# Seams between the sublayers of a fused two-block transformer kernel: the order of sums, squares and splits

## Chip, core and metric

The kernel runs on one core of one Trainium2 chip. The metric is device time in microseconds (us), the median over several executions. TensorE is called PE here, VectorE DVE, ScalarE ACT, GpSimd POOL and SyncE SP, as the profile does.

## What is computed

A residual stream `h` of 256 tokens by 1024 columns goes through two blocks of two layers each, all in 32-bit precision. Cut to what matters:

```python
# first block, per layer l of 2
h = h + 0.5 * swiglu(rmsnorm(h, g0), Wg, Wu, Wd)          # feed-forward, 1024 -> 2816 -> 1024
h = h + mixer_1(rmsnorm(h, g1))                           # four attentions, gated and merged
h = h + 0.5 * swiglu(rmsnorm(h, g2), Wg, Wu, Wd)
h = rmsnorm(h, final_g)                                   # after layer 1
# second block, per layer i of 2
h = h + 0.5 * rmsnorm(swiglu(rmsnorm(h, g0), ...), g1)
h = h + rmsnorm(mixer_2(rmsnorm(h, g2)), g3)              # i=0 dilated attention, i=1 retention
h = h + 0.5 * rmsnorm(swiglu(rmsnorm(h, g4), ...), g5)
```

So there are twelve normalised inputs, p = 0 to 11, and twelve sublayers. A **seam** here is the stretch from the last matmul of one sublayer to the full run of the next; seam p is named by the norm in it. Norms 0, 2, 3, 5, 6, 8, 9, 11 feed a feed-forward (FFN); 1, 4 feed the first block's mixer, 7 the dilated attention, 10 the retention. Seams 1, 3, 4 follow an FFN of the first block, 6 follows it with the final norm between, 7, 9, 10 follow an FFN of the second block, 2 and 5 a mixer of the first block, 8 and 11 a mixer of the second.

## The kernel before, in words

**Weights.** 299 slots of 128 x 3072 floats stream through a ring of four slots (`ring`), loaded by SP; a slot is loaded again once `ring_used` has counted its last use. A matmul at single-pass speed takes operands in a short float form, so each weight w is split in two: the high part `ring_hi` (a rounding copy on ACT, `take_high`, L1444, in an FFN L1480 and L1492) and the low part `ring_lo` = w - high, written over the weight itself (a subtraction on DVE, `take_low` L1772, in an FFN L1821 and L1841). PE multiplies high by high, high by low and low by high. `ring_hi` has two places. Semaphores `hi_ready` and `lo_ready` count split slots in order; PE waits for `lo_ready` in `split_weights` (L796).

**FFN.** Each of 22 slots holds a tile of gate, of up and of down weights. For slot g PE does `gate_up` (L847, 32 matmuls into banks 4 to 7 by turns) and `down` of slot g-1 (L861, 12 matmuls, accumulated over all slots into banks 0 to 3; bank n holds token half n // 2, column half n % 2). ACT and DVE turn each gate/up result into the hidden tile in between (`tile` in ACT's `ffn`, L1470, and in DVE's, L1814). At its end `tile(g)` also splits the first two thirds of slot g+2, so the last two tiles split those of the next sublayer's first two slots: L1492 on ACT, L1841 (128 x 2048) on DVE, which waits for it. If the next sublayer is a mixer, the last third of these two slots is split by `take_high_back` (L1450) and `take_low_back` (L1778), inside the norm.

**Norm.** The gain-scaled, not yet normalised input is transposed; the row factor r = 1/sqrt(mean of squares) is applied to the results later. In the order of each engine's queue:
- DVE `add_output` (L1851; first block) adds banks 0, 1, 2, 3 to `h` (L1857), 512 columns of one token half at a time, each counted in `h_ready`. In the second block ACT squares each bank (`square_outputs`, L1506), DVE multiplies it by the gain (L1872), sums the squares per token half (L1863, `mean_of_output`), POOL takes the power -0.5 for each half (L2430, `output_roots`), and DVE adds to `h` (L1878) in the order of banks 0, 1, 2, 3. The final norm does the like in place (L2043).
- PE `norm` (L821) transposes `h` by column pairs kp = 0 to 3, 16 transposes (L831); kp 0 and 1 wait for `h_ready` at 4p-1 (three adds), kp 2 and 3 for 4p.
- ACT `norm` (L1452) squares token half 0 (L1457, 128 x 1024), makes the high part of the input in eight copies (L1466), then squares half 1.
- DVE `norm` (L1781) makes the low part in eight steps (L1789), splits the back third of the first slot if there is one, waits for both squares, makes the mean `h_sq` (L1794), waits for POOL's root `r_tok` (L2424), builds two diagonals `diag` (L1797), and splits the back third of the second slot.
- PE `root_row` (L838) multiplies a block of ones by `diag`, which gives r as a row in all partitions; DVE `copy_row` (L1802) copies it. In an FFN it stands after the first `gate_up`, into bank 3, then come four fills of banks 0 to 3 with zeros (L883), the fourth after a wait for that copy.

In the two mixers of the second block projection pieces go to banks 6 and 7 by turns (`tile_piece`, L1201). Piece g waits until piece g-2 has been copied out (`piece_bank_2`, L1196), and the copies need the row of r; `root_row` stands after the second piece.

Of the kernel before, what the change touches and what calls it, by code (L numbers as in the profile page):

```python
# [15 lines left out]
P = 128  # L16
SEQ = 256
# [149 lines left out]
def build(nc, stream, x_rows, norm_gT_2, gains_2, table_2, pick_2, ret_const, decay, norm_gT, mla_gT, sinks, posT, lam, subln, table_1, consts, flip_dram, pick_1, out):  # L167

    ctx = ExitStack()
    with ctx:  # L170
# [40 lines left out]
        diag = sb("diag", [P, TT, P])  # L211
# [115 lines left out]
        diag_ready = sem("diag_ready")  # L327
# [108 lines left out]

        def mix_slot(l):
            return l * C_LAYER + C_FFN
# [25 lines left out]

        def dilated_copy(g):


            n, bank = (g - PIECES_DIL) % 8, ps[:, 6 + g % 2, :]
# [16 lines left out]
        def retention_copy(g):  # L485
            what, bank = RET_PIECES[g - PIECES_RET], ps[:, 6 + g % 2, :]
# [295 lines left out]
        def _(pe):  # L782
# [38 lines left out]
            def norm(p, banks):  # L821
# [16 lines left out]
            def root_row(p, bank):  # L838


                pe.wait_ge(diag_ready, p + 1)
                pe.matmul(ps[:, bank, 0:SEQ], ones[:, :], diag[:, :, :].rearrange("p t c -> p (t c)"),
                          start=True, stop=True).then_inc(row_psum, 1)

            def ffn(f, c0, p, last_of_all=False):

                def gate_up(c, t, i=None, first=False):  # L847
                    split_weights(c, i)
                    for part in range(2):
                        for k in range(KD):  # L850
# [10 lines left out]
                def down(c, t, i=None, final=False):  # L861
                    v = FT * f + (c - c0) + 1
                    pe.wait_ge(hidden_ready, v if i is None else NS * i + v)
                    for tt in range(TT):
                        for half in range(2):
                            cols = slice(2 * D + half * 512, 2 * D + half * 512 + 512)
                            x_hi, x_lo = (x[:, t % 2, tt * P:(tt + 1) * P] for x in (hid_hi, hid_lo))
                            for x, w in ((x_hi, high(c)), (x_hi, low(c)), (x_lo, high(c))):
                                last = pe.matmul(ps[:, tt * 2 + half, :], x, w[:, cols], start=False,  # L869
                                                 stop=final and x is x_lo, skip_group_check=True)  # L870
                            if final:
                                last.then_inc(part_ready, 1)
# [1808 lines left out]
```

## Time and profile before

| | us |
|---|---|
| median of 3 runs | 2924.21 (2923.81 to 2926.12) |
| the profiled execution: its time | 2919.25 |
| the profiled execution: its span | 2917.4 |
| PE busy | 2802.2 (96%) |
| DVE / ACT / POOL busy | 1788.1 (61%) / 1342.5 (46%) / 88.6 (3%) |
| mean granted clock of PE | 0.992 |

Durations below come from the profiled execution. Its times are counted from the start of the span; the 1.85 us between span and time lie around it. PE runs at a granted clock of 1.00 (2.4 GHz) or 0.50 (1.2 GHz) in the windows read here.

### The profile page before, as it was taken

How to read it: one execution, taken by the hardware profiler on the slowest of the kernel's cores; microseconds unless marked ns; L12 is line 12 of the kernel's file. 1: busy time of each engine (PE TensorE's matmuls, PEld its weight loads, DVE VectorE, ACT ScalarE, POOL GpSimd, SP SyncE). 2: the span in 40 equal slices, each digit the busy share in tenths (PEclk: the TensorE clock that was granted, in tenths of full speed). 3: DMA queues.
4: the chain of work that ended last, by engine and by line, in shares of the span. 5: the costliest groups of instructions: out<-in, count | busy, mean ns of one | idle time of the engine just before them, and what ended most of it. 6: DMA issues, size and time to landing. Idle time of an engine off the chain costs nothing.

```text
span 2917.4 us, 41161 instructions
## 1 busy us (share of the span) xinstructions
PE 2802.2 (96%) x16502; PEld 2388.7 (82%) x16502; DVE 1788.1 (61%) x2753; ACT 1342.5 (46%) x1937; POOL 88.6 (3%) x135
## 2 busy tenths in 40 slices
PE   7999999999999999999999989998999998999998
PEld 6888988688788888877878879996887887986787
DVE  5665566366666656645666665554666666652665
ACT  4553444254554444424545544444545554451444
POOL 1000000000000000000001001110000000000000
PEclk9999999999999999999999999999999999999999
DMA  6554333444454543335545444453454554434453
GB/s 238 194 189 155 139 147 131 152 168 181 170 190 179 191 148 136 131 145 212 194 173 190 180 169 165 158 166 130 172 191 152 194 189 157 167 137 151 154 191 122
DMA packets 49042, 488.40 MB, mean 167 GB/s; under 512 B 6480, under 2 KB 6576, under 8 KB 10520
## 3 DMA queue, kind: packets, MB, share of 16 engines
q1 hardware_dynamic: 43192, 470.44, 43.7%
q0 software_dynamic: 5728, 16.25, 1.9%
q8 instruction: 87, 1.43, 0.2%
q14 instruction: 35, 0.29, 0.0%
HBM read 485.47 MB, written 1.19 MB: 167 GB/s over the span
## 4 chain that ended last, share of the span: by engine, by line
PE 87%; DVE 7%; ACT 4%; issue 2%; DMA 1%; POOL 0%; DVEq 0%; ACTq 0%; POOLq 0%
PE ps L815 67%; PE ps L869 15%; DVE ring_lo L1772 2%; ACT ring_hi L1444 2%; PE ps L831 1%; PE ps L1084 1%; DMA norm_g<-norm_gT_dram 1%; DVE ring_lo L1841 1%; PE ps L1280 1%; PE ps L1294 0%; PE ps L1189 0%; ACT ring_hi L1492 0%; DVE h L1878 0%; DVE xn L1872 0%; PE ps L883 0%
## 5 line engine op out<-in xcount | busy, mean ns | idle before, releaser
L815 PE MATMUL ps<-uT,ring_hi 128*128 128x512 f32 (+1 forms) x5536 | 1518.2, 345 | 33.3 <-DVE qkT L1893 12.5
L815 PE MATMUL ps<-uT,ring_lo 128*128 128x256 f32 x4176 | 1177.4, 282 | 0.0
L815 PEld LDWEIGHTS ps<-uT,ring_hi 128*128 128x128 f32 x5536 | 957.5, 191 | 190.9 <-issue 21.4
L815 PEld LDWEIGHTS ps<-uT,ring_lo 128*128 128x128 f32 x4176 | 795.5, 190 | 6.2
L1841 DVE TENSOR_TENSOR ring_lo<-ring,ring_hi 128x2048 fp32r<-128x2048 f32 x174 | 398.8, 2292 | 240.4 <-ACT ring_hi L1492 240.4
L1772 DVE TENSOR_TENSOR ring_lo<-ring,ring_hi 128x3072 fp32r<-128x3072 f32 (+1 forms) x100 | 297.0, 2971 | 170.9 <-ACT ring_hi L1444 170.8
L1444 ACT ACTIVATE ring_hi<-ring 128x3072 fp32r<-128x3072 f32 (+1 forms) x100 | 245.9, 2459 | 323.2 <-PE ps L815 232.5
L1492 ACT ACTIVATE ring_hi<-ring 128x2048 fp32r<-128x2048 f32 x174 | 330.6, 1900 | 0.0
L869 PE MATMUL ps<-ring_hi,hid_hi 128*128 128x512 f32 x704 | 276.8, 393 | 9.7 <-DVE hid_lo L1836 9.7
L1482 ACT ACTIVATE work_all<-ps 128x512 f32<-128x512 f32 x176 | 105.3, 598 | 374.8 <-PE ps L815 374.8
L869 PE MATMUL ps<-ring_lo,hid_hi 128*128 128x512 f32 x704 | 275.9, 392 | 0.0
L869 PE MATMUL ps<-ring_hi,hid_lo 128*128 128x512 f32 x704 | 274.0, 389 | 0.0
L815 PE MATMUL ps<-ring_hi,uT 128*128 128x384 f32 (+1 forms) x1024 | 259.5, 333 | 3.4 <-DVE ring_lo L1772 1.8
L1821 DVE TENSOR_TENSOR ring_lo<-ring,ring_hi 128x1024 fp32r<-128x1024 f32 x176 | 214.5, 1219 | 0.5 <-ACT ring_hi L1480 0.5
L1485 ACT ACTIVATE work_all<-work_all 128x256 f32<-128x256 f32 x176 | 73.5, 418 | 271.6 <-DVE work_all L1829 271.6
L815 PEld LDWEIGHTS ps<-ring_hi,uT 128*128 128x128 f32 x1024 | 184.1, 189 | 5.4 <-DVE ring_lo L1772 4.4
L1480 ACT ACTIVATE ring_hi<-ring 128x1024 fp32r<-128x1024 f32 x176 | 183.7, 1044 | 0.0
L815 PE MATMUL ps<-ring_lo,uT 128*128 128x384 f32 (+1 forms) x512 | 169.5, 331 | 0.0
L869 PEld LDWEIGHTS ps<-ring_hi,hid_hi 128*128 128x128 f32 x704 | 132.1, 188 | 43.8 <-DVE hid_lo L1836 13.1
L869 PEld LDWEIGHTS ps<-ring_hi,hid_lo 128*128 128x128 f32 x704 | 132.2, 188 | 29.1
L1826 DVE TENSOR_TENSOR work_all<-ps,work_all 128x512 f32<-128x512 f32 x176 | 121.5, 691 | 51.3 <-ACT work_all L1482 50.8
L869 PEld LDWEIGHTS ps<-ring_lo,hid_hi 128*128 128x128 f32 x704 | 132.2, 188 | 21.0
(272 smaller groups left out, 2465.9 us busy)
## 6 DMA issues: line engine op xcount, KB each, us to landing
ring<-stream_dram SPq DMA_DIRECT2D x299, 1536.0 KB, 6.4
mlaT_all<-bias_vectors POOLq DMA_DIRECT2D x32, 96.0 KB, 2.8
bias<-gains_dram POOLq DMA_DIRECT2D x5, 512.0 KB, 7.5
yR<-bias_vectors POOLq DMA_DIRECT2D x1, 2048.0 KB, 11.0
mlaT_all<-bias_vectors POOLq DMA_DIRECT2D x32, 64.0 KB, 3.2
row<-ret_const_dram POOLq DMA_DIRECT2D x1, 1280.0 KB, 5.6
h<-x_rows_dram POOLq DMA_DIRECT2D x2, 512.0 KB, 11.5
yR<-gains_dram POOLq DMA_DIRECT2D x2, 512.0 KB, 10.0
```

The costliest lines, as they stand in the source:

```text
L815: m = pe.matmul(out_, lhsT, rhs, start=start, stop=stop, **kw)
L831: last = pe.transpose(ps[:, banks[kp], j * SEQ + tt * P:j * SEQ + tt * P + P], h[:, tt, k * P:(k + 1) * P], ident)
L869: last = pe.matmul(ps[:, tt * 2 + half, :], x, w[:, cols], start=False, stop=final and x is x_lo, skip_group_check=True)
L1444: act.activation(split_part(c, high(c)), split_part(c, ring[:, c % NS, :]), ACT.Copy)\
L1480: act.activation(high(c)[:, 2 * D:3 * D], ring[:, c % NS, 2 * D:3 * D], ACT.Copy).then_inc(down_hi, 1)
L1482: act.activation(gu_low, ps[:, 4 + 2 * (g % 2):6 + 2 * (g % 2), SEQ:2 * SEQ], ACT.Copy)\
L1485: act.activation(sil[:, g % 2, :], gu[:, g % 2, 0, :], ACT.Silu).then_inc(silu_ready, 1)
L1492: act.activation(high(c)[:, 0:2 * D], ring[:, c % NS, 0:2 * D], ACT.Copy).then_inc(hi_ready, 1)
L1772: dve.tensor_tensor(split_part(c, ring_lo[:, c % NS, :]), split_part(c, ring[:, c % NS, :]), split_part(c, high(c).bitcast(F32)), ALU.subt ...
L1821: dve.tensor_tensor(ring_lo[:, c % NS, 2 * D:3 * D], ring[:, c % NS, 2 * D:3 * D], high(c)[:, 2 * D:3 * D].bitcast(F32), ALU.subtract)
L1826: dve.tensor_tensor(gu[:, g % 2, :, :], ps[:, 4 + 2 * (g % 2):6 + 2 * (g % 2), 0:SEQ], gu_low, ALU.add).then_inc(gu_summed, 1)
L1841: dve.tensor_tensor(ring_lo[:, c % NS, 0:2 * D], ring[:, c % NS, 0:2 * D], high(c)[:, 0:2 * D].bitcast(F32), ALU.subtract).then_inc(lo_rea ...
```

## The change

The work is the same but for two squares' engines and the way the row of r is made. The parts:
- The last tile of an FFN no longer splits the front of the next sublayer's second slot on DVE. A new `take_low_late` does it inside the next norm, behind the mean (seams 1, 3, 4, 6, 7, 9, 10). ACT's half stays where it was.
- The last step of a sublayer and the adds go by column halves, banks 0, 2, 1, 3, in the first block (`bank_order`, q < 5); in the second block and in the final norm only the adds into `h` do. PE's first transposes wait for two adds.
- In `add_normed` the sum of squares goes ahead of the second product of its token half.
- ACT squares half 0 behind its eight copies; DVE squares half 1 itself (`tensor_tensor_reduce`).
- `diag` is gone: `root_row` multiplies `r_tok`, broadcast along its columns as the stationary operand, by the identity, twice 128 columns instead of once 256. In an FFN it goes to bank 7, after the four fills; the wait for the copy moves to the second half of `gate_up` where t == 1.
- In the second block's mixers pieces 2 and 3 go to banks 0 and 1, so the first four pieces wait for no copy.
- The first store of the output waits for three adds instead of two.

```diff
@@ PE norm, root_row, ffn
-                        pe.wait_ge(h_ready, 4 * p - (kp < 2))
+                        pe.wait_ge(h_ready, 4 * p - 2 * (kp < 2))
...
-                pe.wait_ge(diag_ready, p + 1)
-                pe.matmul(ps[:, bank, 0:SEQ], ones[:, :], diag[:, :, :].rearrange("p t c -> p (t c)"),
-                          start=True, stop=True).then_inc(row_psum, 1)
+                pe.wait_ge(r_ready, p + 1)
+                for tt in range(TT):
+                    last = pe.matmul(ps[:, bank, tt * P:(tt + 1) * P], r_tok[:, tt:tt + 1].to_broadcast([P, P]), ident,
+                                     start=True, stop=True)
+                last.then_inc(row_psum, 1)
...
+                        if part and t == 1:
+                            pe.wait_ge(row_ready, p + 1)
...
+                    for n in bank_order(p) if final else range(4):
+                        tt, half = n // 2, n % 2
...
-                root_row(p, 3)
                 for b in range(4):
-                    if b == 3:
-                        pe.wait_ge(row_ready, p + 1)
                     pe.matmul(ps[:, b, :], zero_bf[:, :], zero_bf[:, 0:1].to_broadcast([1, 512]),
                               start=True, stop=False, skip_group_check=True)
+
+                root_row(p, 7)
@@ bank_order, the pieces of the second block
+            return (0, 2, 1, 3) if q < 5 else (0, 1, 2, 3)
...
+            n = g - (PIECES_DIL if g < PIECES_RET else PIECES_RET)
+            return ps[:, n - 2 if n in (2, 3) else 6 + g % 2, :]
...
+            return None if n < 4 else g - 4 if n < 6 else g - 2
@@ ACT norm
-                square(0)
                 for k in range(KD):
...
-                square(1)
+
+                act.activation(xn[:, 0, :], h[:, 0, :], ACT.Square, accum_out=h_sq[:, 0:1]).then_inc(h_squared, 1)
@@ DVE norm
+            def take_low_late(c):
+
+
+                dve.wait_ge(hi_ready, SPLIT_INDEX[c] + 1)
+                dve.tensor_tensor(ring_lo[:, c % NS, 0:2 * D], ring[:, c % NS, 0:2 * D],
+                                  high(c)[:, 0:2 * D].bitcast(F32), ALU.subtract).then_inc(lo_ready, 1)
...
-                dve.wait_ge(h_squared, 2 * (p + 1))
+                link(dve.tensor_tensor_reduce(xn[:, 1, :], h[:, 1, :], h[:, 1, :], 1.0, 0.0, ALU.mult, ALU.add,
+                                              accum_out=h_sq[:, 1:2]))
+                dve.wait_ge(h_squared, p + 1)
                 dve.tensor_scalar(h_sq[:, :], h_sq[:, :], 1.0 / D, EPS, ALU.mult, ALU.add).then_inc(h_mean, 1)
-                dve.wait_ge(r_ready, p + 1)
-                for tt in range(TT):
-                    last = dve.tensor_scalar(diag[:, tt, :], ident, r_tok[:, tt:tt + 1], None, ALU.mult)
-                last.then_inc(diag_ready, 1)
+                if late is not None:
+                    take_low_late(late)
                 for c in backs[1:]:
                     take_low_back(c)
@@ DVE ffn, add_output, add_normed
-                    if c + 2 < N_SLOTS:
+                    if g < FT - 1 and c + 2 < N_SLOTS:
...
-                for n in range(4):
+                for i, n in enumerate(bank_order(q)):
                     tt, cols = n // 2, slice(512 * (n % 2), 512 * (n % 2) + 512)
-                    dve.wait_ge(part_ready, 4 * q + n + 1)
+                    dve.wait_ge(part_ready, 4 * q + i + 1)
...
-                    dve.wait_ge(y_squared, 4 * j + n + 1)
-                    dve.scalar_tensor_tensor(xn[:, tt, cols], ps[:, n, :], factor, gain[:, cols], ALU.mult, ALU.mult)
                     if n % 2:
                         mean_of_output(j, tt)
-                for tt in range(TT):
+                    else:
+                        dve.wait_ge(y_squared, 4 * j + n + 1)
+                    last = dve.scalar_tensor_tensor(xn[:, tt, cols], ps[:, n, :], factor, gain[:, cols], ALU.mult, ALU.mult)
...
+                for n in (0, 2, 1, 3):
+                    tt, cols = n // 2, slice(512 * (n % 2), 512 * (n % 2) + 512)
                     dve.wait_ge(ry_ready, 2 * j + tt + 1)
-                    for cols in (slice(0, 512), slice(512, 1024)):
-                        dve.scalar_tensor_tensor(h[:, tt, cols], xn[:, tt, cols], r_y[:, tt:tt + 1], h[:, tt, cols],
-                                                 ALU.mult, ALU.add).then_inc(h_ready, 1)
...
-                norm(3 * l + 1, norm_g[:, l, 1, :], backs=(c, c + 1))
+                norm(3 * l + 1, norm_g[:, l, 1, :], late=c + 1, backs=(c, c + 1))
@@ POOL, the stores
-                pool.wait_ge(h_ready, 4 * 11 + 2 * tt + 2)
+                pool.wait_ge(h_ready, 4 * 11 + tt + 3)
```

## Rows read from the trace of the kernel before

**Rows 1.** PE's waits, by what released them: us in total, times, longest.
```profile
PE ps L831 <- DVE h L1878: 22.7, 5, 5.2
PE ps L815 <- DVE qkT L1893: 12.5, 15, 2.0
...
PE ps L831 <- DVE h L1857: 7.3, 3, 2.5
```

**Rows 2.** Timeline of seam 1: start, us, engine, instruction, idle before.
```profile
208.97 0.40 PE L869 MATMUL ps<-ring_hi,hid_lo 128*128 128x512 f32 x1
...
209.72 2.29 DVE L1841 TENSOR_TENSOR ring_lo<-ring,ring_hi 128x2048 fp32r<-128x2048 f32 x1 [1.38 <-ACT ring_hi L1492]
...
211.03 0.39 PE L869 MATMUL ps<-ring_hi,hid_lo 128*128 128x512 f32 x1
211.93 2.48 DVE L1857 SCALAR_TENSOR_TENSOR h<-ps,h 128x512 f32<-128x512 f32 x4
...
213.87 1.97 PE L831 MATMUL ps<-cst,h 128*128 128x128 f32 x16 [2.45 <-DVE h L1857]
```

**Rows 3.** Timeline of seam 2, after a mixer, and of the first tiles behind it.
```profile
583.38 1.97 PE L831 MATMUL ps<-cst,h 128*128 128x128 f32 x16
...
588.17 0.17 DVE L1794 TENSOR_SCALAR h_sq<-h_sq 128x2 f32<-128x2 f32 x1
...
591.46 0.59 PE L842 MATMUL ps<-diag,ones 128*128 128x256 f32 x2
...
592.95 0.50 PE L815 MATMUL ps<-uT,ring_hi 128*128 128x512 f32 x1
...
597.17 2.29 DVE L1841 TENSOR_TENSOR ring_lo<-ring,ring_hi 128x2048 fp32r<-128x2048 f32 x1 [1.38 <-ACT ring_hi L1492]
...
598.71 0.40 PE L869 MATMUL ps<-ring_hi,hid_hi 128*128 128x512 f32 x1
```

**Rows 4.** Timeline of seam 3, PE's transposes and root row.
```profile
776.01 3.55 PE L831 MATMUL ps<-cst,h 128*128 128x128 f32 x16 [2.43 <-DVE h L1857]
...
784.95 0.59 PE L842 MATMUL ps<-diag,ones 128*128 128x256 f32 x2
```

**Rows 5.** One us of seam 3: busy shares, granted clock, DMA share, GB/s.
```profile
777.00:778.00 1.00, 1.00 (x7) 1.00 (x6) 0.00 (x0) 0.83 (x2) 0.00 (x0) 0.50 1.00 160
```

**Rows 6.** Timeline of seam 9: DVE, ACT, POOL and PE's first transposes.
```profile
2224.39 0.58 ACT L1506 ACTIVATE ps<-ps 128x512 f32<-128x512 f32 x1
...
2224.52 2.29 DVE L1841 TENSOR_TENSOR ring_lo<-ring,ring_hi 128x2048 fp32r<-128x2048 f32 x1 [1.38 <-ACT ring_hi L1492]
...
2224.91 0.18 ACT L1506 ACTIVATION_READ_ACCUMULATOR ps<-ps 128x1 f32 x1
...
2226.73 1.28 DVE L1872 SCALAR_TENSOR_TENSOR xn<-ps,bias 128x512 f32<-128x512 f32 x2
...
2228.16 0.56 POOL L2430 TENSOR_TENSOR r_y<-y_sq,half_neg 128x1 f32<-128x1 f32 x1 [186.22 <-DVE y_sq L1863]
...
2229.26 2.73 DVE L1878 SCALAR_TENSOR_TENSOR h<-xn,r_y,h 128x512 f32<-128x512 f32 x4
2229.42 0.98 POOL L2430 TENSOR_TENSOR r_y<-y_sq,half_neg 128x1 f32<-128x1 f32 x1 [0.71 <-DVE y_sq L1863]
...
2231.38 3.67 PE L831 MATMUL ps<-cst,h 128*128 128x128 f32 x16 [5.17 <-DVE h L1878]
```

**Rows 7.** Timeline of seam 10: first square and product, the mean, PE's third piece.
```profile
2422.54 0.58 ACT L1506 ACTIVATE ps<-ps 128x512 f32<-128x512 f32 x1
...
2423.92 1.28 DVE L1872 SCALAR_TENSOR_TENSOR xn<-ps,bias 128x512 f32<-128x512 f32 x2
...
2435.02 0.16 DVE L1794 TENSOR_SCALAR h_sq<-h_sq 128x2 f32<-128x2 f32 x1
...
2439.25 0.47 PE L815 MATMUL ps<-uT,ring_hi 128*128 128x256 f32 x2 [1.19 <-DVE qkT L1893]
```

**Rows 8.** Timeline of the dilated attention: a product with a sum, 512 columns.
```profile
1766.94 0.68 DVE L1918 CUSTOM_DVE_ANT_0 xn<-ps,mlaT_all 128x512 f32<-128x512 f32 x1
```

More of the change, by code:

```diff
@@ L485, in retention_copy @@
         def retention_copy(g):
-            what, bank = RET_PIECES[g - PIECES_RET], ps[:, 6 + g % 2, :]
+            what, bank = RET_PIECES[g - PIECES_RET], piece_psum_2(g)
             if what[0] == "qk":
@@ L863, in down @@
                     pe.wait_ge(hidden_ready, v if i is None else NS * i + v)
-                    for tt in range(TT):
[L865 to L872, printed above, removed]
+                    for n in bank_order(p) if final else range(4):
+                        tt, half = n // 2, n % 2
+                        cols = slice(2 * D + half * 512, 2 * D + half * 512 + 512)
+                        x_hi, x_lo = (x[:, t % 2, tt * P:(tt + 1) * P] for x in (hid_hi, hid_lo))
+                        for x, w in ((x_hi, high(c)), (x_hi, low(c)), (x_lo, high(c))):
+                            last = pe.matmul(ps[:, n, :], x, w[:, cols], start=False,
+                                             stop=final and x is x_lo, skip_group_check=True)
+                        if final:
+                            last.then_inc(part_ready, 1)
                     if not final:
@@ L1184, in out_project @@
                         pe.wait_ge(blocks[0], blocks[1] + k)
-                    for tt in range(TT):
-                        for half in range(2):
-                            cols = slice((k % 3) * D + half * 512, (k % 3) * D + half * 512 + 512)
-                            if k == nk - 1:
-                                pe.matmul(ps[:, tt * 2 + half, :], lhs(k, tt), slot(c)[:, cols],
-                                          start=False, stop=True).then_inc(part_ready, 1)
-                            else:
-                                mm(ps[:, tt * 2 + half, :], lhs(k, tt), slot(c)[:, cols], k == 0, False)
+                    for n in bank_order(q) if k == nk - 1 else range(4):
+                        tt, half = n // 2, n % 2
+                        cols = slice((k % 3) * D + half * 512, (k % 3) * D + half * 512 + 512)
+                        if k == nk - 1:
+                            pe.matmul(ps[:, n, :], lhs(k, tt), slot(c)[:, cols],
+                                      start=False, stop=True).then_inc(part_ready, 1)
+                        else:
+                            mm(ps[:, n, :], lhs(k, tt), slot(c)[:, cols], k == 0, False)
                     if k % 3 == 2 or k == nk - 1:
@@ L1196, in piece_bank_2, with tile_piece @@
             def piece_bank_2(g):
-                s, v = piece_copied(g - 2)
-                pe.wait_ge(s, v)
-                return ps[:, 6 + g % 2, :]
-            def tile_piece(g, c, t, needs=None, bank=None):
-                bank = piece_bank_2(g) if bank is None else bank
+                if piece_before_2(g) is not None:
+                    pe.wait_ge(*piece_copied(piece_before_2(g)))
+                return piece_psum_2(g)
+            def tile_piece(g, c, t, needs=None):
+                bank = piece_bank_2(g)
                 for k in range(KD):
@@ L1233, in dilated_pieces @@
                         pe.wait_ge(lo_back, 2 * DEPTH + n // 3 + 1)
[L1234 to L1237 removed]
+                    if n < 6:
+                        tile_piece(g, c, n % 3, KD * p if hp == 0 and n == 0 else None)
                     else:
@@ L1452, in norm @@
             def norm(p, gain, residues=False):
-                def square(tt):
-                    if p:
-                        act.wait_ge(h_ready, 4 * p - 2 + 2 * tt)
-                    act.activation(xn[:, tt, :], h[:, tt, :], ACT.Square,
-                                   accum_out=h_sq[:, tt:tt + 1]).then_inc(h_squared, 1)
                 if p == 0:
                     act.wait_ge(h_in, 16 * H_DMAS)
-                square(0)
                 for k in range(KD):
```

52 lines of the change are left out of this document (26 added, 26 removed).

## The prediction

> **What bounds the kernel.** I read the page first: PE is busy for 2802.2 of 2917.4 us, DVE for 61% and ACT for 46% (the table of the profile). So the kernel is a queue of matmuls, and only what leaves PE idle, or slows its clock, can be won. The list of PE's waits comes next [rows 1]: the transposes at L831 wait 22.7 us for the second block's adds and 7.3 for the first block's; L815 waits 12.5 for copies at L1893. All the L831 waits lie in the twelve seams, so I read these in the timeline.
>
> Seam 1 shows the pattern [rows 2]. PE starts its last down matmul at 211.03, but the first add starts at 211.93, right behind the low part of the next second slot (2.29 us, from 209.72). The first bank's own last matmul is the one of 208.97; nine follow in 2.06 us, 0.23 apart, so the adds could run beside them. PE starts its transposes at 213.87, after three adds. Seam 2 is the clean case [rows 3]: no slot is split there and PE's transposes follow without a wait. From their start at 583.38 to the root row at 591.46 it is 8.08 us.
>
> The clock adds to this. At seam 3 the wait is 2.43 us, the 16 transposes take 3.55 instead of 1.97 us and the root row comes 8.94 us behind their start [rows 3, 4]: the granted clock there is 0.50, which is 1.2 GHz [rows 5].
>
> **Part 1, low part moved, sums by column halves (first block: seams 1, 3, 4).** The adds start when banks are ready. A bank comes every 0.69 us and an add takes 0.62 (2.48 for four); the second of four adds ends before PE's last matmul is issued (211.03 + 0.23 = 211.26), so the transposes start at 211.26 instead of 213.87: 2.6 us each, 7.8 together. The fourth add ends near 212.15 (last bank 211.26, an estimated 0.25 to see it, 0.62 for the add), when the first eight transposes, half of 1.97 us, are through: no second wait. With no idle stretch, seams 3 and 4 should keep 2.4 GHz as seam 2 does: 8.94 - 8.08 = 0.86 each, 1.7 together (seam 4 taken as seam 3). At seams 2 and 5 two adds instead of three save 0.1 each, since PE had no wait.
>
> **Part 2, seam 6.** The tail is that of seam 1 and all four adds end 2.25 us earlier (214.41 to 212.15 in seam 1's times); the squares and the mean of the final norm follow them. Two adds into h instead of three save 0.68 (2.73 us for four [rows 6]), but the second add now is the one that needs POOL's second root, which at seam 9 takes 0.98 us while an add runs and 0.56 alone [rows 6]; so I give 0.6 of it back. 2.2 us.
>
> **Part 3, second block after an FFN (seams 7, 9, 10).** At seam 9 the first square starts at 2224.39 and is over with the read of its sum at 2225.1, so the first product could start at 2225.2; it starts at 2226.73, behind L1841 [rows 6]. From first product to first add is 2.53 us with the same instructions in another order, from first add to transposes now two adds, 1.4 us, not three. New start of the transposes 2229.2 instead of 2231.38: 2.1 us. At seams 7 and 10 ACT does a back third before its squares: first square at 2422.54, product at 2423.92 instead of 2423.3 [rows 7]. 0.6 + 0.68 = 1.3 us each. Together 4.7. The second root runs beside a product that reads one operand from PSUM and should take 0.56.
>
> **Part 4, after a mixer (seams 8, 11).** No low part was in the way. Two adds instead of three: 0.6 each, 1.2.
>
> **Part 5, the mean and the row.** Square 1 moves to DVE. The nearest row is 0.68 us for a product with a sum over 512 columns [rows 8], so 1.3 us for 1024, between 1.2 and 2. The mean stands 4.8 us behind the transposes' start [rows 3] and goes to 6.1. Then comes the part that speaks against the change. Before, DVE sat still while POOL made the root. Now the 2.29 us low part starts at once, reading two SBUF operands. POOL's 0.98 against 0.56 us stands beside an add of two SBUF operands that starts at 2229.26, and POOL is done some 0.4 us after that add ends [rows 6]: I read it as held up until DVE's instruction ends. So the root is there 2.3 + 0.4 us behind the mean, not 0.9.
> - FFN seams 3, 6, 9: root at 6.1 + 0.1 + 2.3 + 0.4 = 8.9; PE comes to it at 8.08 and the four fills, 1.49 - 0.59 = 0.9, so 9.0. A tie: I charge 0.1 each, 0.3. Seams 0, 2, 5, 8, 11: L1821 holds it up for 1.2 only, free.
> - Seams 7 and 10: PE meets the root row after two pieces. At seam 10, left at its old time, the mean at 2435.02 goes to 2436.3, the low part ends at 2438.7, the root at 2439.1, PE goes on at 2439.7. Before, it went on at 2439.25 after 1.19 us of waiting for a copy [rows 7]. The copy wait goes (banks 0 and 1), the root's wait replaces it: a loss of 0.5 each, 1.0 together.
> - Seams 1 and 4: ACT's first row copy needs the root about 10 us in, 0.8 late on ACT, which PE doesn't wait for.
>
> The Trainium skill (SBUF — State Buffer, Who interferes with whom) has it as an exclusive lock: a DVE instruction with two SBUF inputs and a POOL instruction that reads SBUF, the later one blocked for the whole of the earlier. By that rule the sum stands; by a mere 0.4 us of slowing seams 7 and 10 would gain about 1.0 each instead, 3 us more in all.
>
> **The rest.** Fills and row in an FFN take 1.49 us (591.46 to 592.95 [rows 3]); the fourth fill hardly waits, so the new order gives 0.05 each, 0.4. The broadcast operand isn't in the trace: at best as the old one (0), at worst the old step once more (0.6 x 12 = 7); I take 0, since the same number of columns moves. DVE's first tile in an FFN runs 1 us later: its L1841 ended at 599.46, and PE needs it after the down step that starts at 598.71 and takes 2.75 (12 of 0.229), at 601.46 [rows 3]; so 1.0 us remains. The last store loses 0.2, as both now go out together.
>
> **Sum.** 7.8 + 1.7 + 0.2 + 2.2 + 4.7 + 1.2 - 0.3 - 1.0 + 0.4 - 0.2 = 16.7; with 0.3 for shorter slow stretches at seams 7 and 9, where 5.17 us of idling shrink to 3: **17.0 us**. The profiled execution (2919.25) would take 2902.2, the median of the runs shown, which is 5 us above it, **2907.2**.
>
> **Rivals.**
> - A, POOL isn't held up and the clock stays high in the second block too. 3 us from POOL, and up to 0.86 at each of six seams, 5 us: 25 us faster, 2899. For: seam 2's clean clock. Against: idling of 3 us is left in seams 6 to 11, and 2.43 us was enough at seam 3. 0.17.
> - B, the clock falls anyway at seams 3 and 4 (and 1), and POOL loses to the next DVE instruction as well (1.22 us more at five seams). 17 - 0.86 x 3 - 1.22 x 5 = 8.3 us faster, 2916. For: L1821 and L1778 stand right behind the low part. Against: POOL's root ran during the second of four adds [rows 6]. 0.15.
> - C, the gain is eaten elsewhere, below the 0.2% (5.8 us) that a measurement of this kernel can tell from no change: the broadcast operand costs its 7 us and B holds in part: 2920. 0.07.
> - D, slower. DVE now has 3.6 us more in the norm (1.3 + 2.29) ahead of the first FFN tile. PE needs the second slot's low part 9.5 us behind the transposes' start (592.95 - 583.38 [rows 3]), it is there at 8.5, and 1.0 us is left for the third slot's. If the sum over 1024 columns took over 2.2 us, each us beyond would stop PE at seven seams; at 5.5 us it costs 7 x 3.3 = 23 and more than undoes the gain: 2930. The 0.68 us row speaks against it. 0.03.
>
> **Numbers.** My case has 0.58, 2903 to 2911. With A and B at the ends the range is 2897 to 2915. Faster by over 0.2% is my case, A and B and some of the unsaid, 0.91; within it 0.06; slower 0.03.
>
> **What would show it.** L831's waits for L1857 near zero, those for L1878 from 22.7 to about 13; L1857's first add beside the last down matmuls; granted clock 1.00 through seams 1, 3 and 4; 8.1 us from L831 to the first fill there; L2424 at some 2.7 us instead of 0.70 at seven of twelve; PE waiting at the root row for POOL in seams 7 and 10, nowhere for L1893's first copies. I am wrong if the root takes 0.7 beside the low part, if PE waits for `ring_lo` in a second slot, or if the clock still falls at seams 3 and 4.

## The result, and the profile after

| | before | after |
|---|---|---|
| median, us | 2924.01 (2918.59 to 2926.12, 4 runs) | 2903.20 (2901.78 to 2903.87, 4 runs) |
| the profiled execution: time / span | 2919.25 / 2917.4 | 2901.78 / 2900.0 |
| PE / DVE / ACT / POOL busy | 2802.2 / 1788.1 / 1342.5 / 88.6 | 2798.5 / 1795.7 / 1328.2 / 104.0 |
| mean granted clock | 0.992 | 0.994 |

The ratio is 0.9937, 95% interval 0.9924 to 0.9949: faster by 0.6%. The forecast was 2907.2, in a range of 2897 to 2915. Between the profiled executions the gain is 17.4 us of span where 17.0 stood; between the medians it is 20.8.

In the changed kernel L831 is now L845 (transposes), L842 is L857 (root row), L815 is L829, L869 is L887 (down), L1857 is L1870 and L1878 is L1897 (sums into `h`), L1893 is L1912 (copies of pieces), L2424 is L2443 (root) and L2430 is L2449 (roots of the output).

PE's waits, of the whole kernel (total us, times, longest), to be held against [rows 1]:

```profile
PE ps L845 <- DVE h L1897: 17.0, 7, 3.9
...
PE ps L829 <- DVE qkT L1912: 9.9, 11, 2.5
...
PE ps L857 <- POOL r_tok L2443: 3.1, 2, 1.7
```

The first block's waits for sums (7.3 us before) have gone from the list, the second block's have shrunk from 22.7 to 17.0, and a new one stands at the root row, for POOL.

Seam 1, timeline (start, us, engine, instruction, idle before), answering to [rows 2]:

```profile
208.86 0.50 PE L887 MATMUL ps<-ring_hi,hid_hi 128*128 128x512 f32 x1 [1.22 <-DVE hid_lo L1849]
...
209.86 2.76 DVE L1870 SCALAR_TENSOR_TENSOR h<-ps,h 128x512 f32<-128x512 f32 x4 [1.05 <-PE ps L887]
...
211.50 0.40 PE L887 MATMUL ps<-ring_hi,hid_lo 128*128 128x512 f32 x1
211.73 2.04 PE L845 MATMUL ps<-cst,h 128*128 128x128 f32 x16
```

The sums run beside the down matmuls, and the transposes follow the last of these by 0.23 us, PE's own pace, where it was 2.84. Seams 3 and 4 look the same. Granted clock, in stretches of two us right behind the transposes' start, and at 523 us in one of three inside the first attention (columns: stretch, length, busy us of PE, PEld, DVE, ACT, POOL, then the granted clock, DMA's share, GB/s), answering to [rows 5]:

```profile
212.00:214.00 2.00, 1.90 (x17) 1.54 (x15) 1.38 (x3) 1.63 (x5) 0.00 (x0) 1.00 0.97 344
523.00:526.00 3.00, 3.00 (x19) 3.00 (x19) 1.38 (x6) 0.42 (x1) 0.00 (x0) 0.64 0.00 0
773.00:775.00 2.00, 1.90 (x16) 1.54 (x15) 1.38 (x3) 1.64 (x5) 0.00 (x0) 1.00 0.82 326
963.00:965.00 2.00, 1.90 (x16) 1.54 (x15) 1.38 (x3) 1.66 (x5) 0.00 (x0) 1.00 0.75 270
1518.00:1520.00 2.00, 1.76 (x8) 1.76 (x9) 2.00 (x4) 0.61 (x2) 0.00 (x0) 0.50 0.26 49
2217.00:2219.00 2.00, 2.00 (x11) 1.96 (x10) 1.53 (x4) 1.58 (x4) 0.00 (x0) 0.50 0.65 117
```

1.00 at seams 1, 3 and 4; still 0.50 at 6 and 9, where PE idled 2.66 and 2.92 us first. The stretch at 523 us stands behind a wait of 2.71 us for the latent tiles; behind the same wait of 2.71 us the kernel before had 1.00 in its profile.

Seam 9 and seam 10, timeline, answering to [rows 6, 7]:

```profile
2212.52 0.69 DVE L1888 SCALAR_TENSOR_TENSOR xn<-ps,bias 128x512 f32<-128x512 f32 x1 [1.98 <-ACT ps L1512]
...
2213.23 0.39 PE L887 MATMUL ps<-ring_hi,hid_lo 128*128 128x512 f32 x1
...
2214.64 0.54 POOL L2449 TENSOR_TENSOR r_y<-y_sq,half_neg 128x1 f32<-128x1 f32 x1 [0.71 <-DVE y_sq L1876]
...
2215.07 2.73 DVE L1897 SCALAR_TENSOR_TENSOR h<-xn,r_y,h 128x512 f32<-128x512 f32 x4
...
2216.53 2.75 PE L845 MATMUL ps<-cst,h 128*128 128x128 f32 x13 [2.92 <-DVE h L1897]
...
2418.17 0.40 PE L829 MATMUL ps<-uT,ring_hi 128*128 128x256 f32 x2
...
2419.24 0.17 DVE L1809 TENSOR_SCALAR h_sq<-h_sq 128x2 f32<-128x2 f32 x1
...
2419.31 2.28 DVE L1791 TENSOR_TENSOR ring_lo<-ring,ring_hi 128x2048 fp32r<-128x2048 f32 x1
2419.48 2.67 POOL L2443 TENSOR_TENSOR r_tok<-h_sq,half_neg 128x2 f32<-128x2 f32 x1 [9.31 <-DVE h_sq L1809]
...
2422.21 0.71 PE L857 MATMUL ps<-cst,r_tok 128*128 128x128 f32 x4 [1.36 <-POOL r_tok L2443]
2422.68 0.48 PE L829 MATMUL ps<-uT,ring_hi 128*128 128x256 f32 x2
```

At seam 9 the first product now starts before PE's last down matmul, and the second root takes 0.54 us, now that it stands beside a product that reads PSUM. At seam 10 POOL's root takes 2.67 us for two numbers per partition, and is over 0.56 us after DVE's subtraction: PE waits 1.36 us for it. In the kernel before, the same root at seam 10 took 0.70 us:

```profile
2435.26 0.70 POOL L2424 TENSOR_TENSOR r_tok<-h_sq,half_neg 128x2 f32<-128x2 f32 x1 [7.66 <-DVE h_sq L1794]
```

The next table shows where the 17.4 us come from, by the timelines of both kernels. Its left part is the time from the last down matmul to the first transpose, its right part the time from there to the first full matmul behind the root row (and the fills, in an FFN). The clock named is that behind the transposes' start, before / after:

| seam | to the transposes | gain | from there on | gain | clock |
|---|---|---|---|---|---|
| 1 | 2.84 -> 0.23 | 2.6 | 24.32 -> 24.40 | -0.1 | 1.0 / 1.0 |
| 3 | 2.81 -> 0.23 | 2.6 | 10.44 -> 9.54 | 0.9 | 0.5 / 1.0 |
| 4 | 2.82 -> 0.23 | 2.6 | 20.34 -> 19.22 | 1.1 | 0.5 / 1.0 |
| 6 | 6.44 -> 4.01 | 2.4 | 10.49 -> 11.67 | -1.2 | 0.5 / 0.5 |
| 7 | 5.56 -> 4.26 | 1.3 | 12.30 -> 12.45 | -0.2 | 0.5 / 0.5 |
| 8 | PE's wait alone: 3.55 -> 2.90 | 0.7 | 10.50 -> 9.62 | 0.9 | 0.5 / 1.0 |
| 9 | 5.56 -> 3.30 | 2.3 | 11.42 -> 10.54 | 0.9 | 0.5 / 0.5 |
| 10 | 5.53 -> 4.26 | 1.3 | 10.68 -> 11.15 | -0.5 | 0.5 / 0.5 |
| 11 | PE's wait alone: 3.65 -> 2.99 | 0.7 | 10.57 -> 9.59 | 1.0 | 0.5 / 1.0 |

The left gains are 16.4, the right 2.9. Seams 2 and 5 gave 0.1 each on the left (from the mixer's last matmul to the first transpose 0.52 before and 0.43 after) and nothing on the right (9.57 to 9.60 and 9.57 to 9.56). The start lost 0.5 and the end 0.6. That makes 18.4; the 1.0 between this and 17.4 is rounding and what lies inside the sublayers, where the clock fell in places of one execution and not of the other (the first attention took 1.4 us more after the change, the second 1.5 less).

### The profile page after: what moved, and what is told of

Its sections match the earlier page's. It is cut to its first block, busy times and chain, and to the rows that moved or that the text cites. A ratio compares the mean times of both kernels' runs of the same rounds, so it can differ in the third digit from the quotient of the medians.

```text
span 2900.0 us, 41202 instructions
## 1 busy us (share of the span) xinstructions
PE 2798.5 (96%) x16526; PEld 2384.0 (82%) x16526; DVE 1795.7 (62%) x2753; ACT 1328.2 (46%) x1913; POOL 104.0 (4%) x135
## 4 chain that ended last, share of the span: by engine, by line
PE 87%; DVE 6%; ACT 3%; issue 2%; DMA 1%; POOL 0%; DVEq 0%; ACTq 0%; POOLq 0%
PE ps L829 67%; PE ps L887 16%; DVE ring_lo L1778 2%; ACT ring_hi L1456 2%; PE ps L1101 1%; PE ps L845 1%; DMA norm_g<-norm_gT_dram 1%; PE ps L1295 1%; PE ps L1309 1%; PE ps L1206 0%; DVE xn L1888 0%; DVE uT L1802 0%; PE ps L898 0%; PE ps L953 0%; DVE h L1897 0%
## 5 line engine op out<-in xcount | busy, mean ns | idle before, releaser
L829 PE MATMUL ps<-uT,ring_hi 128*128 128x512 f32 (+1 forms) x5536 | 1516.1, 345 | 30.6 <-DVE mlaT_all L2334 10.9
L829 PE MATMUL ps<-uT,ring_lo 128*128 128x256 f32 x4176 | 1176.4, 282 | 0.0
L829 PEld LDWEIGHTS ps<-uT,ring_hi 128*128 128x128 f32 x5536 | 955.4, 190 | 185.8 <-DVE ring_lo L1778 18.2
L829 PEld LDWEIGHTS ps<-uT,ring_lo 128*128 128x128 f32 x4176 | 794.4, 190 | 6.2
L1854 DVE TENSOR_TENSOR ring_lo<-ring,ring_hi 128x2048 fp32r<-128x2048 f32 x167 | 382.8, 2292 | 230.8 <-ACT ring_hi L1498 230.8
L887 PE MATMUL ps<-ring_hi,hid_hi 128*128 128x512 f32 x704 | 276.8, 393 | 9.8 <-DVE hid_lo L1849 9.8
L887 PE MATMUL ps<-ring_lo,hid_hi 128*128 128x512 f32 x704 | 276.0, 392 | 0.0
L887 PE MATMUL ps<-ring_hi,hid_lo 128*128 128x512 f32 x704 | 274.0, 389 | 0.0
L829 PE MATMUL ps<-ring_hi,uT 128*128 128x384 f32 (+1 forms) x1024 | 258.9, 332 | 3.4 <-DVE ring_lo L1778 1.8
L1834 DVE TENSOR_TENSOR ring_lo<-ring,ring_hi 128x1024 fp32r<-128x1024 f32 x176 | 214.5, 1219 | 0.5 <-ACT ring_hi L1486 0.5
L829 PEld LDWEIGHTS ps<-ring_hi,uT 128*128 128x128 f32 x1024 | 183.5, 188 | 5.5 <-DVE ring_lo L1778 4.4
L829 PE MATMUL ps<-ring_lo,uT 128*128 128x384 f32 (+1 forms) x512 | 169.2, 330 | 0.0
L887 PEld LDWEIGHTS ps<-ring_hi,hid_hi 128*128 128x128 f32 x704 | 132.1, 188 | 43.9 <-DVE hid_lo L1849 13.1
L887 PEld LDWEIGHTS ps<-ring_hi,hid_lo 128*128 128x128 f32 x704 | 132.2, 188 | 29.1
L887 PEld LDWEIGHTS ps<-ring_lo,hid_hi 128*128 128x128 f32 x704 | 132.2, 188 | 21.0
```

Source lines behind the costliest of these rows:

```text
L829: m = pe.matmul(out_, lhsT, rhs, start=start, stop=stop, **kw)
L887: last = pe.matmul(ps[:, n, :], x, w[:, cols], start=False, stop=final and x is x_lo, skip_group_check=True)
L1834: dve.tensor_tensor(ring_lo[:, c % NS, 2 * D:3 * D], ring[:, c % NS, 2 * D:3 * D], high(c)[:, 2 * D:3 * D].bitcast(F32), ALU.subtract)
L1854: dve.tensor_tensor(ring_lo[:, c % NS, 0:2 * D], ring[:, c % NS, 0:2 * D], high(c)[:, 0:2 * D].bitcast(F32), ALU.subtract).then_inc(lo_rea ...
```

## The experiments

All but two were timed in five rounds beside the kernel before, whose medians were 2922.5 and 2923.6 in the two sessions.

**1. The changed kernel again, as a measure.** No edit.

> The changed kernel once more, as the measure for the three kernels beside it. My theory (the gain is made of shorter tails at the seams): 2903 us, as in its first runs, 0.7% below the kernel before. Rival (a good part of the 20.8 us between the two medians is the scatter of the kernel before, whose four runs went from 2918.6 to 2926.1): the ratio comes out nearer to 0.995, with the changed kernel's own time unchanged. In the profile the granted clock is 1.00 from the transposes to the first fill at seams 1 to 5 in either case, and the place inside the attention where it fell for a moment in one layer of each kernel (after a wait of 2.71 us for the latent tiles) is a matter of chance: it may be there, or not, in either layer, at 1.4 to 1.6 us each time.

Measured: 2901.96 us (2900.8 to 2903.2, 5 runs) against 2922.49 (2918.2 to 2923.9, 12 runs), ratio 0.9933, interval 0.9920 to 0.9947. The gain between medians stands, 20.5 us. The changed kernel's own time is unchanged, and its ratio is not nearer to 0.995: the rival of a scatter that flatters it falls. Seams 1 to 5 had a clock of 1.00 again.

**2. Low part back ahead of the sums.**

```diff
-                    if g < FT - 1 and c + 2 < N_SLOTS:
+                    if c + 2 < N_SLOTS:
...
-                norm(3 * l, norm_g[:, l, 0, :], late=layer_slot(l) + 1 if l else None)
+                norm(3 * l, norm_g[:, l, 0, :])
```

and so at the three other calls of DVE's `norm` that had a `late`.

> The changed kernel with one edit undone: the low part of the next second slot (2.28 us on VectorE) is back in the FFN's last tile, ahead of the sums, and out of the norm. My theory (the move is most of the gain): at seams 1, 3 and 4 the transposes start 2.2 us after PE's last down matmul instead of 0.23, so 2.0 us each, 6.0; with an idle stretch of 2 us the clock may fall again at 3 and 4, 0 to 1.7 more. Seam 6: the final norm starts 2.25 us later, +2.2. First product at +0.98 behind the last down matmul where it stood at +0.25 (seams 7 and 10, 0.7 each) or 0.7 ahead of it (seam 9, 1.6): +3.0. POOL's root takes 0.7 again instead of 2.67, and PE's waits of 1.74 and 1.36 us at the root rows of seams 7 and 10 go: -3.0. Together 8 to 10 us slower than the changed kernel, about 2912. Rival 1 (the order by column halves makes the gain, and the sums were late for another reason): under 3 us slower. Rival 2 (the late low part costs at seven seams what it saves, by way of POOL): no difference at all, within 2 us.

Measured: 2911.74 us (8 runs), ratio 0.9970 (0.9959 to 0.9980), 9.8 us slower than the changed kernel. Both rivals fall. PE's wait at seam 1:

```profile
213.03 2.18 PE L845 MATMUL ps<-cst,h 128*128 128x128 f32 x15 [1.81 <-DVE h L1870]
```

From the last down matmul (210.83) to this it is 2.20 us, as expected. The clock stayed at 1.00 at seams 1, 3 and 4. POOL's twelve roots together fell from 26.7 to 18.3 us, and the waits at the root rows went. But 0.7 us again, as expected for the root, it was at seam 10 alone: at the six others of the seven it took 1.6 us, beside the next split of 1.22 us, which now starts where the late low part did.

**3. Sums by rows.**

```diff
-            return (0, 2, 1, 3) if q < 5 else (0, 1, 2, 3)
+            return (0, 1, 2, 3)
...
-                        pe.wait_ge(h_ready, 4 * p - 2 * (kp < 2))
+                        pe.wait_ge(h_ready, 4 * p - (kp < 2))
...
-                for n in (0, 2, 1, 3):
+                for n in (0, 1, 2, 3):
```

(the last at both places that had it, with the wait for the products' end at n = 0 and the stores' thresholds as before the change).

> The changed kernel with the other half of its first edit undone: banks finished and sums made by rows (0, 1, 2, 3), first transposes behind three sums instead of two, also in the second block. My theory: at seams 1, 3 and 4 the third sum ends 0.2 us behind the last down matmul's issue, 0.2 each; at 2 and 5 the third bank is full before PE is done, 0; seam 6 0.3; seams 7 to 11 one sum more ahead of the transposes, 0.65 each, 3.3. Together 4.2 us slower than the changed kernel (2907), and up to 2 more if the longer idle stretches at seams 8 and 11 bring the low clock back there (0.9 each, as in the kernel before). Rival (the halves matter at every seam, since PE's transposes are what the mean and the row hang on, three sums against two everywhere): 0.6 x 11 = 7 us slower. Rival 2 (nothing, because the low part was the only thing in the way): within 1 us.

Measured: 2907.97 us (5 runs), ratio 0.9958 (0.9944 to 0.9972), 6.0 us slower than the changed kernel. Last down matmul to transposes: 0.49 at seams 1, 3 and 4 (expected 0.43), 5.08, 4.17 and 5.10 at 7, 9 and 10, which is 0.84, 0.87 and 0.89 more than in run 1, where 0.65 was expected. The mechanism is as told, and its size in the second block is a third above the expected one. The first rival's even 0.6 everywhere is refuted by seams 1, 3 and 4, the second by the total.

**4. Late low part only behind POOL's root.**

```diff
                 if late is not None:
+                    dve.wait_ge(r_ready, p + 1)
                     take_low_late(late)
```

> The changed kernel with one wait added: VectorE starts the late low part only when POOL's root is there. My theory (POOL's root, which reads two operands in SBUF, can't run beside VectorE's subtraction of two SBUF operands and takes 2.67 us for that reason): the root takes 0.70 us again at all seven seams; PE's waits at the root row of seams 7 and 10 (1.74 and 1.36 us) go, 3.1 us faster than the changed kernel, 2900; at the FFN seams 3, 6 and 9 the four fills stand ahead of the row anyway and the low part, 0.9 us later, is still there for PE's second tile: 0. Rival 1 (the root is slow for another reason, as the new broadcast operand or code of POOL's that isn't loaded): it stays at 2.67, and since the low part now starts behind it, second slots come 3 us late: slower by 1 to 2 us at each of seven seams. Rival 2 (POOL is freed, but VectorE's later low part stops PE at the FFN seams): gain of 3 at seams 7 and 10, loss of 0.5 to 1 at 3, 6 and 9, net near 0.

Measured: 2899.98 us, ratio 0.9931 (0.9918 to 0.9945), 2.0 us faster than the changed kernel by the medians, 2.3 by the spans. The intervals of the two overlap, so the timeline has to carry the verdict. Seam 10 in it:

```profile
2416.75 0.17 DVE L1809 TENSOR_SCALAR h_sq<-h_sq 128x2 f32<-128x2 f32 x1
2416.99 0.70 POOL L2444 TENSOR_TENSOR r_tok<-h_sq,half_neg 128x2 f32<-128x2 f32 x1 [9.14 <-DVE h_sq L1809]
...
2417.73 2.29 DVE L1791 TENSOR_TENSOR ring_lo<-ring,ring_hi 128x2048 fp32r<-128x2048 f32 x1 [0.82 <-POOL r_tok L2444]
...
2418.43 0.60 PE L857 MATMUL ps<-cst,r_tok 128*128 128x128 f32 x4
```

The root is back at 0.70 us with the same instruction and the same operands, so what made it 2.67 was the subtraction beside it. PE's wait is gone. From the transposes to the matmul behind the row, seam 7 takes 10.41 us (12.79 in run 1) and seam 10 9.58 (10.87); seam 3 stays at 9.59 (9.58): the FFN seams neither gain nor lose. Of these 3.7 us, 2.0 to 2.3 arrive; this profile has the low clock at two more places in the retention. By the Trainium skill (SBUF — State Buffer, Who interferes with whom) the later of the two is blocked for the whole of the earlier. The traces agree: of the 2.67 us in the changed kernel, 2.11 pass until the subtraction ends, and 0.56 follow.

**5. Both edits of the sums undone.** The edits of 2 and 3 together.

> The changed kernel with both edits of the sums undone at once (the low part back ahead of the sums, banks and sums by rows, transposes behind three sums); what is left of the change is the mean (one square on VectorE, both behind the copies), the root row from a broadcast, the banks of the first pieces and the products made ahead of the roots. Theory A (the parts add up): the low part cost 9.8 us (2911.7 against 2902.0) and the rows 6.0 (2908.0 against 2902.0), so 2917.8, and the rest of the change gives 4.7 of the 20.5 us below the kernel before. Theory B (they share a tail: behind a late first sum the third one is late by a whole sum at seams 1, 3 and 4 too, 0.6 instead of 0.25 each, and the longer idling brings back the low clock there, 0.9 at two seams): 2 to 3 us more than the sum, 2920. Theory C (the gain of the order by halves is only open once the low part is away, since before that VectorE has all banks full when it starts): under 2917, nearer to 2915. In the profile, A has 2.84 - 0.05 us from the last down matmul to the transposes at seam 1 and a clock of 1.00 at seams 3 and 4, B the 0.50 of the kernel before.

Measured: 2925.67 us (2919.2 to 2928.0, 11 runs), ratio 1.0002 (0.9993 to 1.0011). What is left of the change is worth nothing by itself, within 3 us either way, and the times that the three theories named were all too low. That nothing is a balance: from the transposes on, seams 7 and 10 take 11.82 and 9.34 us (12.30 and 10.68 before), but the transposes of seams 7 to 11 start 0.2 us later behind the last matmul. The profile of this run, seam 1:

```profile
213.05 2.90 PE L845 MATMUL ps<-cst,h 128*128 128x128 f32 x16 [2.41 <-DVE h L1870]
```

2.80 us from the last down matmul to the transposes, the tail that A and B both had, with the clock low behind it (2.90 us for 16 instead of 2.04). It was low at seam 4 too (3.61) and full at seam 3 (1.97).

Do the two edits add up? By the medians they don't: 9.8 and 6.0 us, against 23.7 for both. But this run was timed in the other session, and medians are a poor base here, since the times of this kernel and of the one before spread over 8 us. By the ratios to the kernel before the costs are 0.0037 and 0.0025, against 0.0069 for both: 18 and 20 us, with intervals of 0.0009 to 0.0014 on each ratio. So 2 us more than the sum, which is what theory B says, is the best reading, and no excess at all is not excluded. The timelines show where some 3 us of it can lie. The tails at seams 1, 3 and 4 are 2.6 us longer here than in run 1, where the edits by themselves give 2.0 and 0.3: 0.3 more at each. And either edit alone leaves PE a wait of 1.9 us or less there, with a clock of 1.00 in its profile; both together leave 2.4, and the clock fell at two of the three. What the clock cost over the whole kernel no run separates: the mean is 0.987 here and 0.993 in run 1, and 0.006 of 2926 us is 17 us, the most that it can have cost (an estimate; it costs nothing while PE idles).

**6. PE kept busy in the waits that are left.**

```diff
+                for n in range({0: 3, 6: 10, 7: 12, 8: 8, 9: 8, 10: 12, 11: 8}.get(p, 0)):
+                    x, w = (hid_hi[:, 0, 0:P], hid_hi[:, :, :].rearrange("p a t -> p (a t)")) if p else \
+                        (ones[:, :], ones[:, 0:1].to_broadcast([P, 512]))
+                    pe.matmul(ps[:, 7, :], x, w, start=True, stop=True, skip_group_check=True)
                 if p == 0:
...
-                    act.activation(ps[:, 4 + n, :], ps[:, n, :], ACT.Square, scale=D ** -0.5,
+                    if n == 3:
+                        act.wait_ge(y_squared, 4 * (q - 5) + 1)
+                    act.activation(ps[:, 4 + n % 3, :], ps[:, n, :], ACT.Square, scale=D ** -0.5,
```

> The changed kernel with idle work for PE in the waits that are left: 8 to 12 multiplications of 512 columns that nobody reads, ahead of the transposes of seams 6 to 11 (1.8 to 2.8 us of the 2.7 to 3.9 that PE waits there), and 3 ahead of seam 0's; the squares of the block's output write three banks in turn to leave the fourth to them. Theory (the low clock follows from PE's idling, and only from it): the granted clock stays at 1.00 through all of the seams 6 to 11, their 16 transposes take 2.04 instead of 2.4 to 3.7 us and from the transposes to the first tile behind the row it is 9.6 us instead of 10.3 to 11.7: 1 to 2 us at seam 6, some 1.0 each at 7, 9 and 10, 0.5 on the mean at 8 and 11 (slow in one profile of two). 4 to 6 us faster than the changed kernel, 2897. Rival (the clock follows something else, as what VectorE and ScalarE draw in the seam, or DMA): clock 0.50 there as before, same time, or slower by what the idle work delays. Rival 2 (the seam's length is set by ScalarE's copies and VectorE's, not by PE): clock 1.00 but under 1 us of gain. The waits of 2.5 to 2.7 us inside the two attentions keep their chance to lower the clock.

Measured: 2896.99 us (5 runs), ratio 0.9912 (0.9898 to 0.9925), 5.0 us faster than the changed kernel by the medians of the two sessions, 6 by the ratios. The two intervals just touch, so here too the timeline has to carry the verdict. The windows behind the transposes' start at seams 6 to 11:

```profile
1517.00:1520.00 3.00, 2.77 (x20) 2.21 (x20) 3.00 (x7) 2.40 (x7) 0.00 (x0) 1.00 0.50 143
1711.00:1714.00 3.00, 2.31 (x17) 1.87 (x18) 2.36 (x5) 2.15 (x5) 0.00 (x0) 1.00 0.51 98
2020.00:2023.00 3.00, 2.54 (x19) 2.26 (x20) 2.70 (x7) 2.08 (x6) 0.00 (x0) 1.00 0.47 98
2213.00:2216.00 3.00, 2.36 (x18) 2.09 (x19) 2.71 (x6) 1.90 (x6) 0.00 (x0) 1.00 0.42 79
2407.00:2411.00 4.00, 3.26 (x26) 3.03 (x27) 3.71 (x8) 2.80 (x8) 0.00 (x0) 1.00 0.40 129
2695.00:2698.00 3.00, 2.83 (x21) 2.43 (x21) 2.64 (x7) 2.47 (x7) 0.00 (x0) 1.00 0.55 156
```

1.00 at all six, with DVE and ACT doing what they did. From the transposes on, seams 6, 8, 9 and 11 take 9.81, 9.66, 9.65 and 9.58 us (run 1: 10.55, 10.76, 10.82 and 10.34). Seam 7 stays at 12.47 with a full clock: there POOL's root is the bound, a wait of 1.74 us. At seams 6 to 11 the transposes start as far behind the last matmul as in run 1, so the idle work cost nothing there, and from there on these seams take 4.4 us less than in run 1. At seam 0 it is 9.99 (10.58 and 11.82 in the two profiles of the changed kernel), but the idle work, 5.5 us of it, made the transposes start 0.7 us later behind the matmul ahead of it (6.27 instead of 5.54 us), so nothing is won at that seam. So the low clock in the seams follows from PE's idling and from nothing else that was left as it was.

**7. Both of the last two.** The edits of 4 and 6.

> The two kernels above that should gain, in one: the late low part only behind POOL's root, and idle work for PE in the waits of seams 6 to 11 and 0. If the gains add up (2.0 on the clock of the device for the one, 3 in its seams 7 and 10, and 4 to 6 for the other): 2894 to 2896, with the root at 0.70 us everywhere, no wait of PE at the root row, clock 1.00 in the seams. If the faster copies at seams 7 and 10 only make PE reach another wait sooner (its third piece, or the mean): 2897 or more.

Measured: 2893.30 us (2890.7 to 2894.8, 4 runs), ratio 0.9898 (0.9883 to 0.9913): the fastest of all, 8.7 us below the changed kernel by the medians (10 by the ratios), a little under the range. Seam 7 takes 10.41 and seam 10 8.57 us from the transposes on.

**8 and 9. The kernel before, profiled twice more,** one run each. No edit.

> The kernel before once more, with a profile of its own. The two medians lie 20.5 us apart, the two profiled executions 17.4. Theory (the profiled execution of the kernel before was one of its quickest, since its idle stretches of 2.4 to 2.5 us at seams 1, 3 and 4 and of 2.5 to 2.7 us in the attentions lower the clock in some executions and not in others): this profile has the low clock at another set of places, among them seam 1 (transposes 2.9 to 3.6 instead of 1.97 us) or a second place in the attentions, and the time lies higher in the measure of these places, 1 to 1.6 us each. Rival (the difference is in DMA or in another engine): the same places at the low clock and a longer time elsewhere.

> The same kernel as the one before it, for a third profile: by the theory again another set of places at the low clock, the time between 2918 and 2926 in the order of their number; by the rival the same set.

Measured: 2924.44 and 2918.68 us. Windows behind the transposes of seams 1, 3 and 4, of the first and then of the second:

```profile
214.00:216.00 2.00, 1.77 (x16) 1.56 (x15) 0.97 (x4) 1.83 (x7) 0.00 (x0) 1.00 0.59 123
777.00:779.00 2.00, 1.73 (x16) 1.73 (x16) 0.98 (x3) 1.84 (x5) 0.00 (x0) 1.00 0.32 61
970.00:972.00 2.00, 2.00 (x10) 2.00 (x11) 0.52 (x2) 1.36 (x5) 0.00 (x0) 0.50 0.51 86
```

```profile
214.00:216.00 2.00, 2.00 (x11) 2.00 (x10) 1.86 (x5) 1.97 (x6) 0.00 (x0) 0.50 1.01 301
776.00:778.00 2.00, 2.00 (x12) 2.00 (x12) 0.96 (x3) 1.80 (x6) 0.00 (x0) 0.59 0.42 92
970.00:972.00 2.00, 1.77 (x15) 1.56 (x14) 1.03 (x3) 1.90 (x6) 0.00 (x0) 1.00 0.64 147
```

The kernel before fell at seams 3 and 4 in its first profile, at 4 alone in the second, at 1 and 3 in the third, behind the same waits of 2.4 us. The rival's same set is refuted. The mean clock was 0.992, 0.989 and 0.991 at 2919.25, 2924.44 and 2918.68 us: the slow one has the lowest, but between the two quick ones the order is not that of the clock. Three profiles are few, but the 28 executions of this kernel that were timed beside the runs of this section carry their mean clock too. The 13 with 0.990 to 0.992 took 2918.2 to 2922.2 us, the 15 with 0.988 or 0.989 took 2922.8 to 2926.4. So the times of the kernel before go with its clock, as the theory has it; the 4 us of scatter within each group stay open.

## Why the prediction was right, and where it was off

**Part 1, the first block: right to a tenth.** 2.6 us each were forecast for the tails of seams 1, 3 and 4, and 2.61, 2.58 and 2.59 came. The start 0.23 us behind the last matmul, with no second wait behind eight transposes, was as worked out, and at seam 1 the fourth sum ended 0.89 us behind that start (212.62 against 211.73), as the estimate had it. Run 2 puts 2.0 of the 2.6 on the low part, run 3 0.26 on the third sum; the 0.3 left shows only with both undone (run 5).

**Its clock term: right here, but not for every execution.** 0.86 each was taken from seam 3 and gave 0.90 there and 1.12 at seam 4, where it was not read by itself. The prediction treated "idle 2.43 us, so 0.50" as fixed. Runs 8 and 9 show a chance: after that wait the clock fell in 5 of 9 cases, and in 2 of 3 in run 5. After waits of 1.9 us or less at these seams it fell in none, in seven profiles (the changed kernel's two and runs 2, 3, 4, 6 and 7).

**Part 2, seam 6: the tail right, the clock not.** 2.2 forecast, 2.4 measured up to the transposes. The second root beside an add took 1.01 us, as assumed. Then 1.2 us were lost again in the profiled execution: before, much of the slow stretch fell into the wait itself (granted clock 0.58 over its last 4 us, then 0.84 up to the first tile behind the row), now it lies where PE works (0.85 over the last 3.6 us of the wait, then 0.75). In run 1 the slow stretch was shorter and seam 6 took 10.55 us from the transposes on, no more than before.

**Part 3, seams 7, 9, 10.** 1.3, 2.1 and 1.3 forecast, 1.3, 2.3 and 1.3 measured. **Part 4:** 0.6 each, 0.7 measured, and besides a clock of 1.00 at both, which was forecast by rival A alone, and for all of 6 to 11; run 1 had it at neither. That is chance again. One sign didn't come: PE's waits for L1878 went from 22.7 to 17.0, not to about 13. That figure didn't follow from the prediction's own parts 3 and 4, whose 5.9 us leave 16.8.

**Part 5, POOL.** The sum over 1024 columns took 1.22 and 0.08 us (1.3 taken). The root took 2.67 (2.7 taken) at seven seams and 1.6 at the five others, beside L1834; PE waited at seams 7 and 10 and at no FFN seam. The charge of 0.5 each was 0.2 and 0.5 in the first pair of profiles. Without the wait, run 4 shows, these seams would have gained 2.4 and 1.3 more, 3.7 together where rival A had 3. Rival B's idea that POOL loses to the next DVE instruction too is refuted: at seam 10, as at the other six, the root ends 0.56 us behind the low part's end, and at the FFN seams L1834, which reads two SBUF operands as well, starts right behind the low part without holding it up again. The late root was free at the FFN seams, as the tie was read: in run 4 seam 3 did not change.

**The small terms.** The broadcast operand cost nothing: the value taken, 0, was right and the bound of 7 far off; transposes to first tile at seams 2 and 5 is within 0.03 of before. The new order of fills and row gave nothing either (0.4 forecast); only the sum of these two was measured, so that a small cost of the one hides a small gain of the other is not excluded. The two sums instead of three at seams 2 and 5 gave the 0.2 that was forecast. The 0.3 for shorter slow stretches at 7 and 9 was 0.9 at seam 9 and can't be told from POOL's wait at 7. **The last store** was mis-sized: from the last matmul to the end of the span it is 10.0 us before and 10.6 after, a loss of 0.6, not 0.2. The last store is issued no later than before behind the last matmul (at 2894.2 now, at 2912.3 before, 4.85 us behind it each time). But the two are now issued 0.7 us apart and the slower one lands after 3.8 us; before, they were issued 1.3 us apart and it landed after 3.1.

**The sum against the profile: in part luck.** 17.0 us were forecast and 17.4 came, but misses of opposite sign stand behind that, these among others: the clock at seams 8 and 11 gave 1.9 that the sum didn't have and seam 9 0.6 more than it had, against that seam 6 lost 1.2 again, and the start and the end lost 0.9 more than forecast. **The sum against the median: the step that failed.** The prediction carried 17.0 us over to the median, from 2924.2 to 2907.2. The changed kernel's median lies 1.4 us above its profiled execution and the old one's 4.8 above its own, so 20.8 us show. That the profiled execution is 5 us quick was read as an offset that the change leaves alone. It goes with the clock instead (runs 8 and 9): the profiled execution was one of those at 0.992. The change removes three waits of 2.4 us after which the clock may fall, and the spread is narrower without them: 2918.2 to 2926.4 us over the runs of the kernel before, 2900.8 to 2903.9 over nine of the changed one. That these three waits are the cause is argued from this, and no run has them alone. **Rival D** needed a sum over 1024 columns of 2.2 us and more; it took 1.3, and PE waited for no second slot's low part. **Rival C** had nothing for it.

## What to carry to other kernels

When an engine is idle at a seam, look at what the instruction that it waits behind is for: preparation for a later step, ahead of the sums, cost 2 us at each seam after an FFN of the first block, and behind them it was free there. Put it where no GpSimd instruction has to run: beside a VectorE instruction with two SBUF operands, POOL's 0.7 us became 2.67, and one wait gave it back. Waits of PE of 2.4 us and more cost more than their length here where the clock fell behind them. Idle multiplications in them gave 4 to 5 us, and such waits should be read as a chance, over several profiles.

## What was not expected of the hardware

- The same wait of 2.4 us was followed by the low clock in 5 of 9 cases of one and the same kernel. Each costs 0.9 to 1.2 us at these seams.
- Eight to twelve multiplications that nobody reads kept the granted clock at 1.00 through six seams that had been at 0.50 in most profiles. The 1.1 us of idling left in five of them did no harm.
- The mean clock of one and the same kernel differs from execution to execution, and its time goes with it: 2918.2 to 2922.2 us at 0.990 to 0.992, 2922.8 to 2926.4 at 0.988 or 0.989. One profile, or a median over few runs, can fall on either side.
- Of two output stores of half a megabyte issued 0.7 us apart the slower took 3.8 us to land, against 3.1 for two issued 1.3 us apart.
